# Differential attention on one core: where TensorE issues the score products of the step after next

## The reference, cut to what matters

```python
def diff_attention_group(q, k, v, pos, layer, lambdas, subln):
    hh, d = DIFF_HEADS, DIFF_HEAD_DIM            # 8 heads, 64
    q = rope(...); k = rope(...)                 # two halves a head
    def block(start, q1b, q2b):                  # 128 queries
        mask = chunk_causal_mask(start, s)
        p1 = masked_softmax(einsum('bqhd,bkhd->bhqk', q1b, k1) * scale, mask)
        p2 = masked_softmax(einsum('bqhd,bkhd->bhqk', q2b, k2) * scale, mask)
        return einsum('bhqk,bkhe->bqhe', p1 - lam * p2, vf)
    o = sweep_query_blocks(block, ...)
    return rms_norm_2(o, subln) * (1.0 - lam_init)
```

## Time and profile before

| what | value |
|---|---|
| median of 3 runs | 2508.94 us |
| profiled execution, its own time | 2508.21 us |
| its span | 2506.4 us |
| PE busy in the span | 2441.0 us (97%) |
| DVE busy | 1297.2 us (52%) |
| ACT busy | 877.8 us (35%) |
| POOL busy | 1057.5 us (42%) |
| granted TensorE clock | 0.99 of full speed |

### The profile page before, as it was taken

The page is one execution under the profiler, slowest core; times in us unless marked ns, Lnnn a source line. Parts: engine busy times, 40 slices in busy tenths (PEclk is TensorE's granted clock), DMA queues, the critical chain, the costliest instruction groups (busy, mean ns, idle before and its releaser), DMA issues.

```text
span 2506.4 us, 30237 instructions
## 1 busy us (share of the span) xinstructions
PE 2441.0 (97%) x11728; PEld 1964.9 (78%) x11728; DVE 1297.2 (52%) x1923; ACT 877.8 (35%) x1378; POOL 1057.5 (42%) x830
## 2 busy tenths in 40 slices
PE   8999999999999999999999999999999889999998
PEld 6877667888888888877778788888888657788887
DVE  4336677633543322395777754686126855433302
ACT  5453346322322222334455433222224454322221
POOL 4323344554444444444232245454454223544442
PEclk9999999999999999999999999999999999999999
DMA  4212122232323233222222223323331012223232
GB/s 151 71 55 78 55 73 90 93 101 93 105 93 101 93 95 100 92 84 67 77 80 68 72 76 107 101 93 98 93 100 55 28 37 85 85 93 101 90 100 80
DMA packets 66672, 213.59 MB, mean 85 GB/s; under 512 B 7905, under 2 KB 12257, under 8 KB 66401
## 3 DMA queue, kind: packets, MB, share of 16 engines
q1 hardware_dynamic: 65520, 208.30, 26.1%
q10 hardware_dynamic: 1008, 3.35, 0.4%
HBM read 205.33 MB, written 2.10 MB: 83 GB/s over the span
## 4 chain that ended last, share of the span: by engine, by line
PE 89%; DVE 8%; ACT 1%; issue 1%; POOL 0%; DMA 0%; DVEq 0%; ACTq 0%; SPq 0%
PE ps L641 25%; PE ps L643 24%; PE ps L642 24%; PE ps L662 1%; DVE T L2246 1%; PE ps L663 1%; PE ps L664 1%; PE ps L1001 1%; PE ps L978 1%; PE ps L768 1%; PE ps L1014 1%; PE ps L759 1%; PE ps L846 1%; DVE A L1961 1%; PE ps L793 1%
## 5 line engine op out<-in xcount | busy, mean ns | idle before, releaser
L612 POOL TENSOR_TENSOR w_lo<-w_raw,w_hi 128x512 fp32r<-128x512 f32 (+4 forms) x822 | 1047.8, 1298 | 1411.9 <-ACT w_hi L1357 1411.7
L641 PE MATMUL ps<-H,w_hi 128*128 128x512 f32 x1880 | 753.6, 401 | 20.7 <-DVEq L2002 9.5
L643 PE MATMUL ps<-H,w_lo 128*128 128x512 f32 x1880 | 735.5, 391 | 0.0
L642 PE MATMUL ps<-H,w_hi 128*128 128x512 f32 x1880 | 735.1, 391 | 0.0
L1357 ACT CAST w_hi<-w_raw 128x1024 fp32r<-128x1024 f32 (+4 forms) x411 | 402.8, 983 | 528.1 <-DMA w_raw<-in_weights_dram 522.1
L641 PEld LDWEIGHTS ps<-H,w_hi 128*128 128x128 f32 x1880 | 354.9, 189 | 113.8 <-issue 25.3
L643 PEld LDWEIGHTS ps<-H,w_lo 128*128 128x128 f32 x1880 | 354.5, 189 | 75.1
L642 PEld LDWEIGHTS ps<-H,w_hi 128*128 128x128 f32 x1880 | 355.2, 189 | 73.0 <-issue 2.2
L641 PE MATMUL ps<-split,w_hi 128*128 128x512 f32 x1012 | 401.9, 397 | 5.3 <-issue 3.3
L643 PE MATMUL ps<-split,w_lo 128*128 128x512 f32 x1012 | 394.6, 390 | 0.0
L642 PE MATMUL ps<-split,w_hi 128*128 128x512 f32 x1012 | 394.1, 389 | 0.0
(11 more groups left out here) (432 smaller groups left out, 2443.9 us busy)
## 6 DMA issues: line engine op xcount, KB each, us to landing
w_raw<-in_weights_dram SPq DMA_DIRECT2D x323, 512.0 KB, 3.6
w_raw<-in_weights_dram SPq DMA_DIRECT2D x48, 448.0 KB, 3.3
w_raw<-in_weights_dram SPq DMA_DIRECT2D x22, 256.0 KB, 2.6
A<-A SPq DMA_DIRECT2D x64, 64.0 KB, 2.0
X<-in_xt_dram SPq DMA_DIRECT2D x4, 512.0 KB, 7.9
out_dram<-H SPq DMA_DIRECT2D x8, 256.0 KB, 2.2
w_raw<-in_weights_dram SPq DMA_DIRECT2D x12, 128.0 KB, 2.0
w_raw<-in_weights_dram SPq DMA_DIRECT2D x6, 192.0 KB, 2.3
```

The source lines that it names most:

```text
L612: sub = nc.gpsimd.tensor_tensor(w_lo[:, p % NS, c], w_raw[:, p % NS, c], w_hi[:, p % NS, c].bitcast(F32), ALU.subtract)
L641: mm_(ps[:, bank, :], r(wh), xh, start=(k == 0), stop=False)
L642: mm_(ps[:, bank, :], r(wh), xl, start=False, stop=False)
L643: mm = mm_(ps[:, bank, :], r(wl), xh, start=False, stop=(k == kt - 1))
```

## The change

In `attend_diff` a step's weight units were cut in two: the first half ran, then `scores(c + 2)`, then the second half, then the transposes of step c. Now all units run first, then `scores(c + 2)`, and right behind them, with no weight block between, the wait for the probabilities and the transposes. Products, sizes, semaphores and the number of units in each step stay; later lines of the file move up by two, so the transposes are L1044 instead of L1046.

```diff
                 for c in range(32):
                     head, i = c // 4, c % 4
-                    n = DIFF_FILL[c % len(DIFF_FILL)]
-                    run(fill, n // 2)
+                    run(fill, DIFF_FILL[c % len(DIFF_FILL)])
                     if c + 2 < 32:
                         scores(c + 2)
-                    run(fill, n - n // 2)
                     pe.wait_ge(s_pn, c + 1)
                     if c:
                         pe.wait_ge(s_pt, c)
```

## The result

The changed kernel takes 2524.23 us, the median of five runs (2518.39 to 2528.77), against 2508.91 for the kernel before (five runs, 2506.70 to 2509.18): a ratio of 1.0066, 95% interval 1.0056 to 1.0077. That is 15 us slower, outside the forecast range (2505.3 to 2514.3) and on the slower side, which had a chance of 12%. The kernel before stays within 3 us here and within some 8 us over all later runs; the changed one spreads over 10.

A forecast was written before the change was run, and what follows sets the result against it. PE was taken to bound the kernel. Terms -0.9 + 0.1 + 0.2 + 2.0 + 0.2 = +1.6 us gave 2509.8 from the profiled execution, 2510.5 from the median; forecast 2510.2 us, range 2505.3 to 2514.3.

The forecast's parts named there:

- What bounds the kernel: Whole kernel: PE is 89% of the 2506.4 us span, its stage losses count one for one; DVE waits 22.2 us for scores.
- The restart: On PE, each step loses one restart of the weight stream: 0.03 us gained a step, 0.9 us for 30 steps.
- The rule named there: On PE, a tiling mode change drains TensorE: two drains a step before and two now, so nothing saved.
- the 0.11 of the row: On PE, distance from a lone transpose to the next product, 0.11 us, taken as nearest price for starting transposes behind masks.
- What DVE needs in the turn of i = 3: DVE, once a head, maxima to probabilities: 4.30 us needed, PE gives 4.24, so 0.06 missing; 4 x 0.06, 0.2 us.
- What is added when DVE is held up.: DVE turns with head_out: hold-ups of 0.80 and 1.16 us, mean 0.33 a turn over six turns, 2.0 us lost.
- My upper bound: For the hold-ups of DVE's turns with head_out: all six at 1.16 us, 7.0 us lost.
- Turn 7 and step 3: DVE behind ropes in turn 7: at most 0.8 us, 0.2 taken; PE at step 3 waits away 0.1 us of savings.
- DVE becomes the bound at each head: Rival: six DVE turns need 4.30 us against 4.24, each hit by a POOL pass for 1.16; 2517 us, chance 12%.
- It decides from about 1 us a turn on: DVE's turns with head_out: the rival of DVE as bound at each head decides from about 1 us a turn.

The follow-up runs named there:

- e3: The kernel before, with the scores moved right to the transposes only in steps with i = 3: 2518.0 us, ratio 1.0050.
- e5: The kernel before, with the scores moved right to the transposes in all steps except those with i = 3: 2508.5 us, ratio 1.0003.
- e1: The changed kernel, with POOL's passes in the attention stage cut to almost nothing and low weight parts left out: 2505.9 us, ratio 0.9992 to the kernel before.
- e2: The kernel before, with POOL's passes in the attention stage cut to almost nothing and low weight parts left out: 2512.8 us, ratio 1.0018.
- e10: The changed kernel run again, unaltered: 2527.0 us, ratio 1.0073 to the kernel before.
- e8: The kernel before, with DVE's maxima of steps 9 and 13 repeated 3 times more, of 21 and 25 4 times more: 2519.8 us, ratio 1.0044.

## Why the prediction was wrong, point by point

- **What bounds the kernel.** Right: PE, one for one, and DVE hanging on the scores (22.2 to 43.1 us; 40 was said).
- **The restart.** Right in kind, half in size: 0.06 a step was measured and 0.03 taken, 1.9 us for 30 steps in place of 0.9. The rule named there, of the Trainium skill, TensorEngine Tiling (Array Packing), counted as two drains before and two now, would have saved nothing, 1.9 us less than was measured; no run here shows a drain by itself. The transposes cost 0.06 behind the masks and not the 0.11 of the row.
- **What DVE needs in the turn of i = 3.** Right: only this turn decides (e3, e5), and the bare turn just fits (e1). Where no pass met it, it cost 0.1 to 0.2 us (steps 12 and 28), where 0.06 was said.
- **"What is added when DVE is held up."** This is the step that failed. I took the two hold-ups of six turns, 0.80 and 1.16, as chance, kept their mean of 0.33 and set 2.0 us. They are not chance. In three of the six turns (15, 19 and 23) a pass of POOL stands 2 to 4 us behind the transposes of the step before, at nearly the same distance in both kernels, since ACT casts behind its copy of them (3.5 and 3.8, 2.2 and 2.3, 2.3 and 2.3 us). Before, all three turns ended just ahead of that pass, by 0.2 to 0.3 us (1394.62 against 1394.81 in turn 19); started later, their ends lie in it, two held-up operations ahead of steps 16 and 24 and four ahead of step 20. The other three turns have no pass there. Steps 16, 20 and 24 then waited 2.1, 3.7 and 1.8 us, 7.9 in all with the small ones. Turns 11 and 15, whose hold-ups I counted, had theirs at the start, from a pass that the late turn no longer meets; step 12 waited 0.1. The rows for the right answer were at hand: where each pass lay against the shifted turn. My upper bound, 1.16 a turn, was taken from turns that touched a pass with one operation, the scaling (0.80 us longer in both; the rest of turn 15's 1.16 is idle time ahead of its reciprocal, which it has in both kernels), and a turn can lie in it with four. In the term's place stand 7.9 us of waits instead of 2.0.
- **The clock** stood in no term of the sum. Half clock behind the waits made 3.4 us of the profiled 11.4, for which the sum had nothing. The median is 15 us up and the profiled execution 11; half clock at the small products, some 8 to 10 us in e3 and e2, most likely makes the times near 2528, but what the median execution (2524.23) lost beyond the profiled one is open.
- **Turn 7 and step 3.** The ropes cost nothing measurable (the probabilities of 8 came 0.10 us ahead of the transposes).
- **The rival "DVE becomes the bound at each head"** was the right one, with 2517 us against 2518 to 2520 in the fastest three executions. Its mechanism was right, its number of turns wrong (three, not six), its price per turn too low (1.2 us against waits of 2.1, 3.7 and 1.8), and it had no clock in it: that its number comes so near is partly luck. "It decides from about 1 us a turn on" held.

## What to carry to other kernels

Slack of a moved wait is not a number but a place: before moving work on one engine by 2 us, lay the shifted turn over the passes of every engine that was seen to hold it up, pass by pass, and look which operations then overlap. An average of collisions before says nothing, when both sides hang on the same event. If something in the turn can be done while the engine waits anyway (head_out here), put it there first, and then move the scores: the two edits together made the stage 1.9 us shorter, where the one alone made it 9.5 us longer and the other changed nothing.

## What the runs showed of the hardware that was not expected

- A chain of small VectorE operations beside four GpSimd instructions in a row went forward one held-up operation per GpSimd instruction: 1.25 us each for operations of 0.29 and 0.35 us, 0.80 for one of 0.16. A reciprocal between them kept its 0.17 us.
- TensorE's clock fell to half with TensorE busy all the time, in a stretch of 128x32 products between weight blocks, in the profiled executions of e3 and e2 and in none of the others, and stayed there for 20.5 and 23.9 us, about 8 to 10 us of time. The times of the same program suggest that it comes in some executions only.
- The clock fell or stayed with waits of 1.8 to 2.6 us in no fixed way: 3.4 us at half clock behind the wait of 1.8 in the changed kernel and behind that of 2.2 in e10, none behind 2.1 in the changed kernel or 2.6 in e8.
